# Normalised activations at 64, 192, 192 and 448 bytes from the weights' place, in place of 320

## The chip, the core and the metric

One core of a Trainium2 chip runs the whole program. The time is the device time of one execution in microseconds: 793.31 us for the kernel before, the median of 3 runs (793.28 to 793.38). All times below come from these runs or from one profiled execution of the same kernel.

## The reference

Input: 256 tokens of width 1024, float32, with 16 meta tokens put in front for the first mixer. Two blocks follow each other.

```python
# first block: h has 16 + 256 rows
a = rmsnorm(h, norm1); proj = a @ w_in           # pool, forgetting and stick-breaking attention
h = h + concat(y_pool, y_fox, y_sb) @ w_out
a = rmsnorm(h, norm2)                            # norm 0 below
h = h + (silu(a @ w_gate) * (a @ w_up)) @ w_down # first FFN, width 2816
h = rmsnorm(h, final_norm)
# second block
h = swiglu(rmsnorm(x, ffn1_pre), w_ffn1_in, w_ffn1_out)   # second FFN, norm 1
x = x + 0.5 * rmsnorm(h, ffn1_post)
h = mixer(rmsnorm(x, mix_pre), w_mix_in, ...)             # convolution and mLSTM, norm 2
x = x + rmsnorm(h, mix_post)
h = swiglu(rmsnorm(x, ffn2_pre), w_ffn2_in, w_ffn2_out)   # third FFN, norm 3
x = x + 0.5 * rmsnorm(h, ffn2_post)
```

## The kernel before

**Numbers in two parts.** Every large product is taken in a reduced float32 format (F32R) from a high and a low part. ScalarE rounds the landed weights `raw` into `whi` (L695), VectorE takes `wlo = raw - whi` (L1023). The activations have `xn_hi` and `xn_lo` in the same way. A product is then three: whi with hi, whi with lo, wlo with hi.

**The weight stream.** All large weights come as 129 units of 128 x 2048 values (1 MB), one after another into three slots (`raw`, `whi`, `wlo`, each three tiles of 8192 bytes per partition). SyncE issues the loads. An FFN has 11 groups of 256 hidden features with a gate, an up and a down unit each. The groups 2 to 10 run in a loop on every engine.

**The matmuls of a group.** Gate unit: 16 products of whi with 512 moving columns (hi and lo parts of 256 tokens side by side, `hi_products`), then 16 of wlo with 256 columns of hi (`lo_products`). Up unit: first its 16 wlo products, then its 16 whi products. So in order of time there are 16 of 512 columns, 32 of 256, 16 of 512. Down unit (`rows_tile`): 24 products of 512 columns, in which the hidden activations `hhi` and `hlo` are the stationary operand and the weights move. Each matmul has its own load of the stationary operand, which the profile shows as PEld. All of them are issued from the helper `mm`, L1478.

**The mixer.** 12 units. Ten are column products (`columns_tile`): for each k tile whi with hi, whi with lo, wlo with hi, 256 columns each. Two units, of kind v, have the activations as stationary operand and the weights moving (`tokens_tile`). Short work of the mLSTM heads stands between units. At the head of each FFN and of the mixer a first unit (`first_paired_unit`, `first_columns_unit`) runs all hi products and then all lo products as the activations arrive.

**Where the activations stand.** `xa` is one tile, 8 x 544 values per partition. In the first stage (projections, `w_in`) it is used as it is: k tile `kt` at 544 x 4 x kt = 2176 kt bytes, hi part first, lo part 1088 bytes on. For the three FFNs and the mixer the same memory is seen as 8 k tiles of 2 x 256 values, 2048 bytes apart, that start a given number of values into `xa`. `XN_AT` holds that number for norm 0 to 3, and L424 cuts the views from it:

```python
for at, far in XN_AT:
    line = xa_line[:, at:at + KT * 2 * SEQ if far == SEQ else at + 2 * far]
    if far == SEQ:
        xn.append(line.rearrange("p (k h c) -> p k h c", k=KT, h=2))
```

The tiles between `whi` and `xa` are whole multiples of 512 bytes, so `whi`, `wlo` and the start of `xa` have one address modulo 512. A stationary block of a column product begins at a multiple of 512 bytes in its slot. With 80 values, an activation block begins 320 bytes on from it, modulo 512, for every k tile. `ya`, `hhi` and `hlo` begin at 0 on the same scale.

Of the kernel before, what the change touches and what calls it, by code (L numbers as in the profile page):

```python
# [41 lines left out]
SEQ = 256  # L42
# [3 lines left out]
GROUPS = FF // 256  # L46
UNIT = 2048
SLOTS = 3
XN_AT = ((80, SEQ),) * 4
XN_HI = (0, 0, 0, 0)  # L50
EPS = 1e-6
NEG = -1e30
# [218 lines left out]
def build_blocks(nc, x_in, meta_in, wstream, ident_in, vecs_in, small_in, const_in, rows_in, out):  # L271
    with ExitStack() as ctx:  # L272
# [150 lines left out]
        xn = []  # L423
        for at, far in XN_AT:  # L424
            line = xa_line[:, at:at + KT * 2 * SEQ if far == SEQ else at + 2 * far]
# [1600 lines left out]
```

## Time and profile before

| | |
|---|---|
| median of 3 runs | 793.31 us |
| the profiled execution | 793.85 us, of which the span from first to last instruction 792.0 |
| TensorE busy | 781.6 us, 99% of the span |
| weight loads (PEld) busy | 687.9 us, 87% |
| VectorE, ScalarE busy | 533.2 us (67%), 429.3 us (54%) |
| granted TensorE clock | 1.000 of full |
| DMA | 141.16 MB, mean 178 GB/s |
| longest group | whi with xa, 1744 matmuls, 377.4 us busy |

In the stages: first stage to 120 us, first FFN loop some 148.6 to 304, second 331 to 486, mixer 504 to 600, third FFN loop 627 to 782. TensorE's rows give the start of an instruction and its length. The length includes the way through the array, so consecutive matmuls overlap in the view. The pace is the distance from one start to the next. A row with x16 holds 16 consecutive matmuls of one form, from the start of the first to the end of the last.

### The profile page before, as it was taken

Reading aid. Unit: us, or ns where it says so; the run is one execution under the profiler, and the core shown is the slowest. Engines: PE = TensorE matmul, PEld = TensorE weight load, DVE = VectorE, ACT = ScalarE, POOL = GpSimd, SP = SyncE. Lnnn points to the kernel's source line nnn. Section 1 sums busy time; section 2 is a strip of 40 time slices with the busy share of each in tenths; the row PEclk is TensorE's granted clock in tenths of the full one; section 3 lists DMA queues with packets and bytes.
Section 4 is the critical chain, followed back from the end, with each engine's and each line's share of the span. In section 5 each row is a group of like instructions: output and inputs, shape, how many; then the busy total and the mean of one; then the engine's idle time right before and its main releaser. Section 6 shows DMA issues by size and latency. Waiting matters only on the chain.

```text
span 792.0 us, 12209 instructions
## 1 busy us (share of the span) xinstructions
PE 781.6 (99%) x4710; PEld 687.9 (87%) x4710; DVE 533.2 (67%) x628; ACT 429.3 (54%) x565; POOL 28.3 (4%) x35
## 2 busy tenths in 40 slices
PE   9999999999999999999999999999999999999997
PEld 8989988888888888888888887999988888888885
DVE  7866657766666667866666566766977766666665
ACT  6556657544544448744544447565557654454444
POOL 0000000000000000000000000002520000000000
PEclk9999999999999999999999999999999999999999
DMA  9633433645555553665545554452444664555521
GB/s 335 235 110 112 143 115 128 245 166 205 191 183 209 175 196 110 238 224 199 198 176 209 183 188 159 142 204 108 161 165 162 221 223 166 205 192 183 208 106 54
DMA packets 20797, 141.16 MB, mean 178 GB/s; under 512 B 2448, under 2 KB 2704, under 8 KB 4384
## 3 DMA queue, kind: packets, MB, share of 16 engines
q1 hardware_dynamic: 20192, 138.65, 48.8%
q0 software_dynamic: 576, 2.10, 0.8%
q8 instruction: 21, 0.34, 0.2%
q14 instruction: 8, 0.07, 0.0%
HBM read 139.69 MB, written 1.05 MB: 178 GB/s over the span
## 4 chain that ended last, share of the span: by engine, by line
PE 94%; ACT 2%; DVE 2%; issue 1%; DMA 1%; SPq 0%; DVEq 0%; ACTq 0%
PE ps L1478 93%; ACT whi L695 1%; PE ps L1484 1%; DMA raw<-wstream 1%; DVE x L1227 0%; ACT squared L710 0%; DVE xa L1034 0%; PE ps L1707 0%; DVE wlo L1023 0%; PE ps L1677 0%; PE ps L1926 0%; DVE xg L1222 0%; DVEq L272 0%; ACT L928 0%; PE ps L1709 0%
## 5 line engine op out<-in xcount | busy, mean ns | idle before, releaser
L1478 PE MATMUL ps<-xa,whi 128*128 128x512 f32 (+2 forms) x1744 | 377.4, 347 | 0.0
L1023 DVE TENSOR_TENSOR wlo<-raw,whi 128x2048 fp32r<-128x2048 f32 x128 | 293.6, 2295 | 82.2 <-ACT whi L695 82.2
L1478 PEld LDWEIGHTS ps<-xa,whi 128*128 128x128 f32 x1744 | 299.6, 188 | 41.4 <-issue 2.1
L695 ACT ACTIVATE whi<-raw 128x2048 fp32r<-128x2048 f32 x128 | 244.2, 1909 | 6.9 <-PE ps L1478 6.8
L1478 PE MATMUL ps<-xa,wlo 128*128 128x256 f32 (+1 forms) x1376 | 219.8, 278 | 0.0
L1478 PEld LDWEIGHTS ps<-xa,wlo 128*128 128x128 f32 x1376 | 187.9, 188 | 2.8
L1478 PE MATMUL ps<-wlo,hhi 128*128 128x512 f32 x240 | 93.5, 390 | 0.0
L1478 PE MATMUL ps<-whi,hlo 128*128 128x512 f32 x240 | 93.5, 390 | 0.0
L1478 PE MATMUL ps<-whi,hhi 128*128 128x512 f32 x240 | 93.5, 390 | 0.0
L889 ACT ACTIVATE hhi<-arena 128x512 fp32r<-128x512 f32 x30 | 19.0, 633 | 88.4 <-PE ps L1478 81.9
L875 ACT ACTIVATE arena<-ps 128x512 f32<-128x512 f32 x33 | 19.7, 597 | 85.5 <-PE ps L1478 85.4
L883 ACT ACTIVATE arena<-ps 128x512 f32<-128x512 f32 x33 | 19.7, 597 | 71.4 <-PE ps L1478 71.4
L1478 PE MATMUL ps<-whi,ya 128*128 128x512 f32 x176 | 56.5, 395 | 0.0
L1478 PEld LDWEIGHTS ps<-whi,hhi 128*128 128x128 f32 x240 | 45.1, 188 | 9.6
L1478 PEld LDWEIGHTS ps<-wlo,hhi 128*128 128x128 f32 x240 | 45.1, 188 | 9.5
L1478 PEld LDWEIGHTS ps<-whi,hlo 128*128 128x128 f32 x240 | 45.1, 188 | 9.5
L1269 DVE TENSOR_TENSOR arena<-ps,arena 128x512 f32<-128x512 f32 x33 | 22.8, 691 | 39.6 <-ACT arena L875 39.6
L1278 DVE TENSOR_TENSOR arena<-ps,arena 128x512 f32<-128x512 f32 x33 | 22.8, 691 | 36.6 <-ACT arena L883 36.6
L1290 DVE TENSOR_TENSOR hlo<-arena,hhi 128x512 fp32r<-128x512 f32 x30 | 20.8, 692 | 37.8 <-ACT hhi L889 37.7
L1478 PEld LDWEIGHTS ps<-whi,ya 128*128 128x128 f32 x176 | 33.1, 188 | 6.8
L1478 PE MATMUL ps<-wlo,ya 128*128 128x512 f32 x88 | 34.5, 393 | 0.0
L1478 PE MATMUL ps<-arena 64*128 64x144 f32 (+11 forms) x190 | 24.3, 340 | 1.8 <-DVE arena L1067 1.3
(221 smaller groups left out, 531.6 us busy)
## 6 DMA issues: line engine op xcount, KB each, us to landing
raw<-wstream SPq DMA_DIRECT2D x128, 1024.0 KB, 4.8
gain_row<-rows_in POOLq DMA_DIRECT2D x4, 512.0 KB, 3.9
x<-x_in SPq DMA_DIRECT2D x2, 512.0 KB, 4.0
raw<-wstream SPq DMA_DIRECT2D x2, 512.0 KB, 5.8
out<-x SPq DMA_DIRECT2D x4, 256.0 KB, 2.1
xg<-const_in SPq DMA_DIRECT2D x1, 912.0 KB, 11.8
small<-small_in SPq DMA_DIRECT2D x1, 152.0 KB, 6.1
arena<-meta_in SPq DMA_DIRECT2D x1, 64.0 KB, 4.5
```

Of the source, the lines that this page charges most:

```text
L695: nc.scalar.activation(whi[slot][:], raw[slot][:], ACT.Copy).then_inc(hi_ready, 1)
L875: nc.scalar.activation(silu, products(4)[1], ACT.Copy).then_inc(gate_lo_out, 1)
L883: nc.scalar.activation(up_sum, products(6)[1], ACT.Copy).then_inc(up_lo_out, 1)
L889: nc.scalar.activation(ya[:, 0:2, 0:SEQ] if last else hhi[:], hact, ACT.Copy).then_inc(hhi_done, 1)
L1023: nc.vector.tensor_tensor(wlo[slot][:], raw[slot][:], whi[slot][:].bitcast(F32), ALU.subtract).then_inc(lo_ready, 1)
L1269: nc.vector.tensor_tensor(silu, products(4)[0], silu, ALU.add).then_inc(gate_out, 1)
L1278: nc.vector.tensor_tensor(up_sum, products(6)[0], up_sum, ALU.add).then_inc(up_out, 1)
L1290: nc.vector.tensor_tensor(lo, hact, hi.bitcast(F32), ALU.subtract).then_inc(hlo_done, 1)
L1478: return nc.tensor.matmul(o, lhsT, rhs, start=start, stop=stop, skip_group_check=True)
L1484: ins = nc.tensor.transpose(turn_place(k, kt)[:, tt * P:(tt + 1) * P], x[:, tt, kt * P:(kt + 1) * P], ident[:])
```

## The change

`XN_AT` gets other numbers. Norm 0 (first FFN) begins 16 values = 64 bytes into `xa`, norm 1 (second FFN) 48 values = 192 bytes, norm 2 (mixer) 192 bytes, norm 3 (third FFN) 112 values = 448 bytes, in place of 320 bytes for all four. The widest view still ends inside the tile (112 + 4096 of 4352 values). The order of instructions on every engine is the same in both kernels; only addresses of reads and writes in `xa` differ.

```diff
-XN_AT = ((80, SEQ),) * 4
+XN_AT = ((16, SEQ), (48, SEQ), (48, SEQ), (112, SEQ))
 XN_HI = (0, 0, 0, 0)
```

## Rows read from the trace of the kernel before

**Rows 1.** The page: busy time, share and instructions; granted clock; chain by engine.
```profile
PE 781.6 (99%) x4710; PEld 687.9 (87%) x4710; DVE 533.2 (67%) x628; ACT 429.3 (54%) x565; POOL 28.3 (4%) x35
...
PEclk9999999999999999999999999999999999999999
...
PE 94%; ACT 2%; DVE 2%; issue 1%; DMA 1%; SPq 0%; DVEq 0%; ACTq 0%
```

**Rows 2.** Window 331 to 486 us, FFN two's loop: busy us by engine, then clock.
```profile
331.00:486.00 155.00, 155.00 (x825) 133.17 (x825) 99.82 (x80) 76.19 (x70) 0.00 (x0) 1.00 0.55 196
```

**Rows 3.** TensorE in order of time (start us, length us), FFN two, group 2.
```profile
338.14 3.84 PE L1478 MATMUL ps<-xa,whi 128*128 128x512 f32 x16
341.82 3.79 PE L1478 MATMUL ps<-xa,wlo 128*128 128x256 f32 x32
345.44 3.82 PE L1478 MATMUL ps<-xa,whi 128*128 128x512 f32 x16
349.10 0.39 PE L1478 MATMUL ps<-whi,hhi 128*128 128x512 f32 x1
...
351.16 0.39 PE L1478 MATMUL ps<-whi,hhi 128*128 128x512 f32 x1
...
354.33 0.39 PE L1478 MATMUL ps<-whi,hlo 128*128 128x512 f32 x1
```

**Rows 4.** The same view, mixer, a unit of column products.
```profile
524.80 0.28 PE L1478 MATMUL ps<-xa,wlo 128*128 128x256 f32 x1
...
526.92 0.28 PE L1478 MATMUL ps<-xa,wlo 128*128 128x256 f32 x1
```

**Rows 5.** The same view, the mixer's two v units.
```profile
511.07 0.28 PE L1478 MATMUL ps<-wlo,xa 128*128 128x256 f32 x1
...
511.78 0.28 PE L1478 MATMUL ps<-wlo,xa 128*128 128x256 f32 x1
...
518.06 0.28 PE L1478 MATMUL ps<-wlo,xa 128*128 128x256 f32 x1
...
518.74 0.28 PE L1478 MATMUL ps<-wlo,xa 128*128 128x256 f32 x1
```

**Rows 6.** The same view, mixer's first unit, then the third FFN's first units.
```profile
499.06 1.98 PE L1478 MATMUL ps<-xa,whi 128*128 128x256 f32 x16
...
608.65 2.05 PE L1478 MATMUL ps<-xa,whi 128*128 128x256 f32 x16
...
612.52 5.66 PE L1478 MATMUL ps<-xa,whi 128*128 128x512 f32 x24
...
620.31 3.93 PE L1478 MATMUL ps<-xa,wlo 128*128 128x256 f32 x32
```

**Rows 7.** TensorE's busy us and instructions (x) in 4 us windows, mixer.
```profile
517.50:521.50 4.00, 4.00 (x38) 1.00 0.12 16
...
552.00:556.00 4.00, 4.00 (x36) 1.00 0.33 117
```

**Rows 8.** TensorE in order of time, first stage, four k tiles' whi pairs.
```profile
32.40 0.41 PE L1478 MATMUL ps<-xa,whi 128*128 128x272 f32 x2
...
32.77 0.42 PE L1478 MATMUL ps<-xa,whi 128*128 128x272 f32 x2
...
33.16 0.41 PE L1478 MATMUL ps<-xa,whi 128*128 128x272 f32 x2
...
33.53 0.42 PE L1478 MATMUL ps<-xa,whi 128*128 128x272 f32 x2
```

**Rows 9.** Groups by form, TensorE: loops of FFN two, three, then mixer.
```profile
L1478 PE MATMUL ps<-xa,whi 128*128 128x512 f32 x296 | 71.0, 392 | 0.0
...
L1478 PE MATMUL ps<-xa,whi 128*128 128x512 f32 x292 | 70.1, 392 | 0.0
...
L1478 PE MATMUL ps<-xa,whi 128*128 128x256 f32 x288 | 52.2, 283 | 0.0
L1478 PE MATMUL ps<-xa,wlo 128*128 128x256 f32 x144 | 40.2, 279 | 0.0
```

## The prediction

> **What bounds the kernel now.** I read the busy times and the clock first, then the chain of waits, then TensorE's instructions in order of time. TensorE is busy 99% of the span at the full granted clock, 2.4 GHz by the row's nines, and the chain lies 94% on it [rows 1]. Inside the loop of the second FFN it never pauses, 155.0 us busy of 155.0 [rows 2], and the other two loops read the same. So neither transfers nor the other engines set the end there. What a matmul costs beside the next one does, and that is the only thing an address can change.
>
> I take that cost from start to start, since the duration shown holds the drain as well. Group 2 of the second FFN [rows 3]: the 16 gate products with whi start at 338.14 and the next kind at 341.82, 3.68/16 = 230 ns each; the 16 up products take 349.10 - 345.44 = 3.66, 228.8 each; mean 229.4 for 512 columns. The 32 products with wlo take 3.62/32 = 113.1 ns for 256 columns. The 14 down products from 351.16 to 354.33 take 226.4 each. By columns, 113.3 and 226.7 look like one floor, and the whi products stand 2.7 ns above it. The third FFN shows the same lengths.
>
> The mixer is different. From 524.80 to 526.92 there are 18 products of 256 columns, 2.12/18 = 117.8 ns each, 4.5 above the floor [rows 4]. The v units show both: 511.07 to 511.78 is 118 each, 518.06 to 518.74 is 113 each, the same instructions and shapes, in two slots whose places differ by whole multiples of 512 bytes [rows 5]. So one pair of addresses has two paces, and what went before decides. The same is seen ahead of the FFNs: 16 whi products take 1.98 us in one place and 2.05 in another, (1.98 - 0.28)/15 = 113.3 and (2.05 - 0.28)/15 = 118.0 [rows 6]. The slow pace is inherited: group 1 of the third FFN has its 32 wlo products in 3.93 us, (3.93 - 0.28)/31 = 117.7, although 32 products of 512 columns stand just ahead; in group 2, behind the first down products, they take 3.79 [rows 3, 6]. In the mixer most stretches are slow: a window of 4 us holds 36 products (four windows, 36 or 37 each), and 38 in the fast v unit and in the first unit [rows 7], the two or so under way at the edge counted.
>
> **Does the address matter, and by what period?** While matmuls stream, the loads of the next weights are under way, 87% of the span [rows 1]: two reads of SBUF side by side. In the first stage each k tile stands 2176 bytes behind the last, so the moving operand's place changes by 128 bytes modulo 256 and also modulo 512. Its pairs of whi products read 0.41, 0.42, 0.41, 0.42 us and so on, alternately over the eight tiles, of which four stand in the rows, and a tile of three products takes 0.37 or 0.39 us in turn [rows 8]. Place therefore matters, with a period of two tiles: 256 bytes, not 512. Then 320 and 64 are one place, and 192 and 448 are one place. This step is read from hundredths of a microsecond, so I hold it at four in five.
>
> **The change part by part.** No instruction, wait or DMA is added, removed or moved. ScalarE and VectorE write the normalised activations to other columns of the same tile, in pieces of the same shape.
> (a) First FFN, 320 to 64: one place by the period. 0.
> (b) Second and third FFN, 320 to 192 modulo 256. Their loops hold 296 + 292 = 588 whi products of 512 columns [rows 9]. No row has such a product at 192. Bounds: the down products' floor, 588 x 2.7 = 1.6 us gained; on the other side, the 16 gate products behind a down unit take 19 ns more than the 16 up products (16 x 1.2), which four openers at some 234 ns would make (an estimate: 229.4 + 19/4); if that pace held throughout, 588 x 4.6 = 2.7 us lost. I take most of the gain, 1.2, because the nearest steady rows at 512 columns are the down products.
> (c) Their 576 wlo products (18 groups of 32 as in rows 3) already run at the floor and cannot gain. If the new place made them inherit the slow pace they would lose 576 x 4.5 = 2.6 us. I take 0, since a down unit at distance 0 still stands ahead of each gate unit, and behind it the products were fast.
> (d) Mixer: 432 of the column products (288 + 144) [rows 9] at 4.5 ns above the floor are 1.9 us. The only rows with operands 192 apart are the v units, which have activations as weights and weights as the moving operand, 64 the other way round: one unit fast, one slow [rows 5]. Half, 0.95. Bounds: all of it gained; or the fast v unit turned slow (48 x 4.5 = 0.2) and each column product as slow as the worse tiles of the first stage, where three products of 272 columns take 0.39 us [rows 8], 130 each against a floor of 120.4, 9.6 above it and 5.1 worse than now: 0.2 + 2.2 = 2.4 lost.
> (e) The openings of the second and third FFN hold some 96 slow products each, 96 x 4.5 = 0.4 us each ([rows 6] show the third's). I leave them, and keep 0.8 for the range.
> Sum: 1.2 + 0.95 = 2.15 us gained. The profiled execution took 793.85 (span 792.0 and 1.85 around it), 0.54 above the median of the runs, 793.31. With the change 791.7 on its own scale, 791.2 on the median's. All bounds of gain together are 1.6 + 1.9 + 0.8 = 4.3, to 789.0.
>
> The Trainium skill speaks against all of this. Its page "TensorE: Matmul & The Clock Gate", section "Step-by-step: what each phase is for", says that TensorE has two independent read ports to SBUF and that loading the next weights takes nothing from the running matmul; "SBUF — State Buffer", section "SBUF: two separate sides", adds that TensorE never waits on anyone there. By that rule the sum would be 0 and the time 793.3. Rows 5 and 8 disagree in part: something in the pair of reads changes a matmul by 4 to 5 ns. They do not show that 192 is better than 64.
>
> **The rivals.**
> A, no effect: only the distance's being an odd multiple of 64 counts, 64 and 192 are mirror images and the two paces go on as they fall. For it: the period of 256, and the v units, which at the mirrored distance have just the two paces that the column products have at 64. Against it: whi products at 64 have a pace of their own (229.4) between the others, which need not be symmetric. Time 793.3, within 0.5 of it. This is also the case that the change does not do what it says, certain for the first FFN if the period holds.
> B, slower: at 192 the wlo products of the second and third FFN lock into the slow pace, as group 1 of the third FFN does today. Place: behind the gate's 16 whi products in each of the 18 loop groups. Price: 2.6 us for (c), with (b) and (d) unchanged: 795.9. It decides from the point where a row of 32 wlo products reads 3.93 instead of 3.79. Against it: the rows in between are wiped clean by each down unit today.
> C, the period is 512 after all, and the first FFN changes too: its loop holds the same 0.8 us above the floor, so with the forecast's gains 790.4.
>
> **How the numbers follow.** A measurement of this kernel tells about 0.2%, 1.6 us, from no change. Forecast case (part of (b) and (d) gained, 789.0 to 792.6): 0.44, of which 0.06 falls short of 1.6 us. C 0.08, faster. A 0.28. B 0.20, of which 0.02 is within 1.6 us. So faster 0.38 + 0.08 = 0.46, same 0.06 + 0.28 + 0.02 = 0.36, slower 0.18. The likeliest time is 791.2. The range is 789.0, all gains, to 796.0, B's price; the forecast case alone is 789.0 to 792.6. Beyond 796.0 lie B together with the losses of (b) and (d).
>
> **What the profile after would show.** The first FFN's rows unchanged: 3.84, 3.79, 3.82 us for 16, 32 and 16 products, or C is right. In the second and third FFN the whi rows at 3.79 to 3.80 in place of 3.84 and 3.82 for (b); the wlo row stays 3.79 or goes to 3.93 (B). In the mixer 38 products in 4 us where 36 or 37 stood for (d). I am wrong in kind if any engine but TensorE shows a changed wait, or if whi products get slower than 229.4 ns.

## The result and the profile after

The changed kernel takes 795.86 us (median of 6 runs, 795.65 to 796.39), the kernel before in the same comparison 793.60 (6 runs, 793.28 to 794.24). The ratio is 1.0029, with a 95% interval of 1.0018 to 1.0039. It is slower by some 2.3 us, where 2.15 us faster was forecast. The profiled execution took 796.36 us with a span of 794.6, which is 2.6 more than the 792.0 of before.

The page of the changed kernel, against [rows 1]: busy times and shares, granted clock, and the chain by engine.

```profile
PE 783.2 (99%) x4710; PEld 686.1 (86%) x4710; DVE 533.3 (67%) x628; ACT 429.4 (54%) x565; POOL 28.3 (4%) x35
...
PEclk9999999999999999999999999999999999999999
...
PE 89%; DVE 6%; ACT 2%; issue 1%; DMA 1%; SPq 0%; POOL 0%; DVEq 0%; ACTq 0%
```

The clock is the same. The chain has moved: PE has 89% of it and DVE 6%, where it was 94% and 2%. TensorE is busy 1.6 us more.

Where the time went is read from four starts of the same matmuls. TensorE in order of time, the kernel before (start us, length us, then the instruction): first product of the second FFN, of the mixer, of the third FFN, and the last product with wlo.

```profile
310.74 0.36 PE L1478 MATMUL ps<-xa,whi 128*128 128x256 f32 x1
...
495.36 0.35 PE L1478 MATMUL ps<-xa,whi 128*128 128x256 f32 x1
...
604.80 0.36 PE L1478 MATMUL ps<-xa,whi 128*128 128x256 f32 x1
...
785.77 0.39 PE L1478 MATMUL ps<-wlo,ya 128*128 128x512 f32 x1
```

The same four in the changed kernel.

```profile
310.99 0.37 PE L1478 MATMUL ps<-xa,whi 128*128 128x256 f32 x1
...
497.01 0.36 PE L1478 MATMUL ps<-xa,whi 128*128 128x256 f32 x1
...
606.16 0.36 PE L1478 MATMUL ps<-xa,whi 128*128 128x256 f32 x1
...
788.36 0.39 PE L1478 MATMUL ps<-wlo,ya 128*128 128x512 f32 x1
```

The differences are 0.25, 1.65, 1.36 and 2.59 us. The first 0.25 is there before any activation of the change is read: the stages up to the first FFN differ by it, and the whole first FFN adds 0.00. The second FFN adds 1.40, the mixer gives back 0.29, the third FFN adds 1.23.

TensorE in order of time in the changed kernel, a group in the loop of the first FFN and group 2 of the second, with the first down product behind each, to be read against [rows 3].

```profile
155.02 3.84 PE L1478 MATMUL ps<-xa,whi 128*128 128x512 f32 x16
158.70 3.79 PE L1478 MATMUL ps<-xa,wlo 128*128 128x256 f32 x32
162.33 3.82 PE L1478 MATMUL ps<-xa,whi 128*128 128x512 f32 x16
165.99 0.39 PE L1478 MATMUL ps<-whi,hhi 128*128 128x512 f32 x1
...
338.54 3.89 PE L1478 MATMUL ps<-xa,whi 128*128 128x512 f32 x16
342.27 3.80 PE L1478 MATMUL ps<-xa,wlo 128*128 128x256 f32 x32
345.91 3.89 PE L1478 MATMUL ps<-xa,whi 128*128 128x512 f32 x16
349.64 0.40 PE L1478 MATMUL ps<-whi,hhi 128*128 128x512 f32 x1
```

First FFN, 64 bytes: 3.84, 3.79, 3.82 as before, and 10.97 us from the first product to the down unit. Second FFN, 192 bytes: 3.89, 3.80, 3.89 and 11.10 us. The 16 whi products take (342.27 - 338.54)/16 = 233.1 ns, and (349.64 - 345.91)/16 = 233.1 ns, where they took 230.0 and 228.8. The row of the 32 wlo products is 0.01 us longer. The third FFN, at 448 bytes, has the same 11.10 us.

The mixer in the changed kernel, same view: the last 16 products of its first unit (whi with the lo part), two places in each v unit, and two 1.70 us apart in a unit of column products.

```profile
500.86 2.05 PE L1478 MATMUL ps<-xa,whi 128*128 128x256 f32 x16
...
512.54 0.28 PE L1478 MATMUL ps<-wlo,xa 128*128 128x256 f32 x1
...
513.25 0.28 PE L1478 MATMUL ps<-wlo,xa 128*128 128x256 f32 x1
...
519.66 0.28 PE L1478 MATMUL ps<-wlo,xa 128*128 128x256 f32 x1
...
520.36 0.28 PE L1478 MATMUL ps<-wlo,xa 128*128 128x256 f32 x1
...
526.21 0.28 PE L1478 MATMUL ps<-xa,wlo 128*128 128x256 f32 x1
...
527.91 0.28 PE L1478 MATMUL ps<-xa,wlo 128*128 128x256 f32 x1
```

It is close to the mirror of [rows 4 to 6]: the column products are fast, the first unit and the second v unit slow; the first v unit was slow before as well. The column products run at (527.91 - 526.21)/15 = 113.3 ns. Both v units run at 118 ns, (513.25 - 512.54)/6 and (520.36 - 519.66)/6, and so does the first unit, 2.05 us for 16. TensorE's waits from 560 to 580 us show where the gain went (engine and line, what it waited for, us in total, times, longest).

```profile
PE ps L1478 <- DVE arena L1389: 0.5, 1, 0.5
PE ps L1478 <- DVE arena L1395: 0.2, 1, 0.2
```

The kernel before has no such wait in that stretch. The longer of the two, TensorE in order of time, first the kernel before, then the changed one:

```profile
577.25 0.60 PE L1926 MATMUL ps<-ident,arena 128*128 128x128 f32 x4
577.61 0.48 PE L1478 MATMUL ps<-whi,ya 128*128 128x512 f32 x1
```

```profile
577.83 0.60 PE L1926 MATMUL ps<-ident,arena 128*128 128x128 f32 x4
578.97 0.50 PE L1478 MATMUL ps<-whi,ya 128*128 128x512 f32 x1 [0.54 <-DVE arena L1389]
```

From start to start it is 0.36 us before and 1.14 after, 0.78 more; the place of the other wait costs 0.31 more. Added up in this way over the whole mixer, the column products take 1.7 us less, the v units 0.3 more and the work between the units 1.1 more. That leaves the 0.29 us.

### The profile page after: what moved, and what is told of

Its sections match the earlier page's. It is cut to its first block, busy times and chain, and to the rows that moved or that the text cites. A ratio compares the mean times of both kernels' runs of the same rounds, so it can differ in the third digit from the quotient of the medians.

```text
span 794.6 us, 12209 instructions
## 1 busy us (share of the span) xinstructions
PE 783.2 (99%) x4710; PEld 686.1 (86%) x4710; DVE 533.3 (67%) x628; ACT 429.4 (54%) x565; POOL 28.3 (4%) x35
## 4 chain that ended last, share of the span: by engine, by line
PE 89%; DVE 6%; ACT 2%; issue 1%; DMA 1%; SPq 0%; POOL 0%; DVEq 0%; ACTq 0%
PE ps L1478 87%; DVE wlo L1023 2%; ACT whi L695 1%; DMA raw<-wstream 1%; PE ps L1484 1%; DVE arena L1444 0%; DVE arena L1455 0%; DVE x L1227 0%; ACT squared L710 0%; DVE xa L1034 0%; PE ps L1707 0%; PE ps L1677 0%; POOL arena L671 0%; DVE ya L1043 0%; DVE arena L1383 0%
```

## Experiments

The distance below is that of the activations from the weights' place, modulo 256 unless it is said otherwise. The loop group is the 64 products of a gate and an up unit, from the first start to the start of the down unit: 10.97 us at 320, 11.10 at 192.

**The mixer alone at 192.**

```diff
-XN_AT = ((80, SEQ),) * 4
+XN_AT = ((80, SEQ), (80, SEQ), (48, SEQ), (80, SEQ))
```

> The three FFNs stay at 320 bytes, the mixer alone goes to 192. Theory 1 (the whi products of 512 columns in the second and third FFN carry the whole loss, and the mixer's gain is given back at waits on VectorE): the mixer's column products run at 113.3 ns, its v units at 118, TensorE waits 0.3 and 0.8 us more on VectorE's L1395 and L1389, and the time is 0 to 0.5 us under the kernel before. Rival (the mixer itself is slower for its waits): 0.5 to 1.5 us over it. Rival (the gain of 1.9 us shows in full once the FFNs are left alone): 1.5 us or more under it.

Measured 793.64 us against 793.69, ratio 0.9998 (0.9989 to 1.0007). TensorE in order of time, second FFN:

```profile
338.26 3.84 PE L1478 MATMUL ps<-xa,whi 128*128 128x512 f32 x16
...
349.23 0.39 PE L1478 MATMUL ps<-whi,hhi 128*128 128x512 f32 x1
```

A wait of TensorE from 494 to 604 us in the same run, beside 2.0 us on `x` that the kernel before has too:

```profile
PE ps L1478 <- DVE arena L1389: 0.5, 1, 0.5
```

The FFN is back at 10.97 us. The mixer has its fast column products (113.3 ns), slow v units (118) and the wait on L1389. So the mixer's part of the change is worth nothing that can be measured, as theory 1 said, and the gain in pace does not become time.

The same run shows something about the two paces. Up to the mixer its instructions and addresses are those of the kernel before. The last 16 products of the first unit of the first FFN, first in the kernel before, then in this run:

```profile
130.19 1.98 PE L1478 MATMUL ps<-xa,whi 128*128 128x256 f32 x16
```

```profile
130.44 2.05 PE L1478 MATMUL ps<-xa,whi 128*128 128x256 f32 x16
```

That is (1.98 - 0.28)/15 = 113.3 ns in one execution and (2.05 - 0.28)/15 = 118.0 in the other. So not even the order of the work together with the addresses fixes which of the two paces is taken in an opening. In the loops all nine groups of an FFN agree within 0.01 us in every run.

**The second and third FFN alone at 192.**

```diff
-XN_AT = ((80, SEQ),) * 4
+XN_AT = ((80, SEQ), (48, SEQ), (80, SEQ), (48, SEQ))
```

> Second and third FFN at 192 bytes, first FFN and mixer at 320 as before. Theory (whi products of 512 columns at 192 carry the whole loss): 11.10 us per group of 64 products in both FFNs, in all 2.4 to 2.9 us over the kernel before, ratio 1.003; the mixer's rows as before. Rival (part of the loss comes from the mixer's new state or from the openings): under 1.5 us over.

Measured 796.91 us against 793.75, ratio 1.0036 (1.0023 to 1.0050). Both FFNs are at 11.10 us per group (second FFN, same view):

```profile
338.10 3.89 PE L1478 MATMUL ps<-xa,whi 128*128 128x512 f32 x16
...
349.20 0.40 PE L1478 MATMUL ps<-whi,hhi 128*128 128x512 f32 x1
```

The two FFNs carry the whole loss; the mixer, from its first product to the third FFN's, takes 109.5 us against 109.4 in the kernel before. The medians differ by 3.2 us, a little over the 2.4 to 2.9 expected; the interval, 1.8 to 4.0 us, holds those. The profiled spans differ by the same 2.6 us as the full change.

**Distance or absolute place.**

```diff
-XN_AT = ((80, SEQ),) * 4
+XN_AT = ((48, SEQ), (48, SEQ), (48, SEQ), (48, SEQ))
+        pad = sb("pad", [P, 32])          # 128 bytes, ahead of whi
         whi = [sb(f"whi{s}", [P, UNIT], F32R) for s in range(SLOTS)]
```

> All four norms at 192 bytes, and an unused tile of 128 bytes ahead of whi, so that weights and activations all stand 128 bytes further on: the activations are at the absolute address modulo 512 that they have at 320 in the kernel before, while the distance is 192. Theory 1 (distance): all three FFN loops at 11.10 us per group of 64 products, whi products at 233.3 ns, time 796.5 to 797. Rival (the absolute place of the moving operand): 10.97 us and 229 ns as in the kernel before, time 793.5.

One run, 797.36 us. A loop group of the first FFN:

```profile
154.69 3.89 PE L1479 MATMUL ps<-xa,whi 128*128 128x512 f32 x16
158.43 3.80 PE L1479 MATMUL ps<-xa,wlo 128*128 128x256 f32 x32
...
165.79 0.40 PE L1479 MATMUL ps<-whi,hhi 128*128 128x512 f32 x1
```

165.79 - 154.69 = 11.10 us, and the whi products take (158.43 - 154.69)/16 = 233.8 ns (233.3 over the nine groups). The other two loops read the same. The activations stood at the address modulo 512 of the kernel before, the weights 128 bytes further on. What counts is the distance, not the place of the activations. 192 and 448 give the same paces, as 320 and 64 do: the period of 256 holds.

**Other distances.** Three runs change `XN_AT` alone: (0, 32, 0, 8) values, (24, 40, 32, 56) and (12, 20, 52, 18).

> First FFN at 0 bytes, second at 128, mixer at 0, third at 32. A loop group's 64 products take 10.97 us at 64 and 11.10 at 192. Theory 1 (the distance of moving from stationary place, modulo 256, sets the pace, with the down products at 0 as the floor): 226.7 ns per product of 512 columns and 10.89 us per group in the first FFN; 128 is open, 10.9 to 11.3; 32, half a step from 0, between the first FFN's value and 10.97. Rival (whi products with hi and lo parts side by side are slower for a reason of their own, and only that differs from the down products): 229 ns in the first FFN as well, 10.97 us. Mixer: theory 1 says 113.3 ns where the pace is not inherited slow.

> First FFN at 96 bytes, second at 160, mixer at 128, third at 224. If the pace rises smoothly with the distance from 64 (229.0 ns) to 192 (233.3), 96 and 160 lie between them, 10.97 to 11.10 us per group of 64 products, and 224 lies over or under 192 as the curve goes back to 0. If only the whole 64-byte block counts, 96 reads as 64 (10.97), 160 as 128 and 224 as 192 (11.10).

> First FFN at 48 bytes, second at 80, mixer at 208, third at 72 from both weights' places. 64 has 10.97 us per group of 64 products, 32 and 96 had 11.24 and 11.32. If 64 is the bottom of a smooth curve, 48, 72 and 80 lie between, 10.97 to 11.3. If only places at a whole 64 bytes are good, all three are at 11.2 to 11.3 us at once. A value under 10.97 would give a better kernel.

| distance, bytes | run | loop group, us |
|---|---|---|
| 0 | first FFN of the first | 11.11 |
| 32 | third FFN of the first | 11.24 |
| 48 | first FFN of the third | 11.26 |
| 64 | kernel before | 10.97 |
| 72 | third FFN of the third | 11.25 |
| 80 | second FFN of the third | 11.24 |
| 96 | first FFN of the second | 11.32 |
| 128 | second FFN of the first | 11.26 |
| 160 | second FFN of the second | 11.24 |
| 192 | changed kernel | 11.10 |
| 224 | third FFN of the second | 11.24 |

They took 801.87, 803.97 and 802.69 us, one run each. There is no curve between 64 and 192, and no neighbour of 64 is good: 48 and 72 are already at the level of 128. The smooth curve of the expectations is out, and so is the reading that every whole 64 bytes is good, since 128 is not. So 64 was the best place of the eleven, and the change had only one way to go in the FFNs. The mixer at distance 0 missed too: its column products take 120.0 ns, where theory 1 had 113.3. The first FFN at distance 0:

```profile
154.86 3.79 PE L1478 MATMUL ps<-xa,whi 128*128 128x512 f32 x16
158.48 4.00 PE L1478 MATMUL ps<-xa,wlo 128*128 128x256 f32 x32
162.31 3.82 PE L1478 MATMUL ps<-xa,whi 128*128 128x512 f32 x16
165.97 0.39 PE L1478 MATMUL ps<-whi,hhi 128*128 128x512 f32 x1
```

The first 16 whi products take (158.48 - 154.86)/16 = 226.3 ns, the floor, as theory 1 said. The other 16, behind the wlo products, take (165.97 - 162.31)/16 = 228.8, as at 64: their first five take 229 to 235 ns, the rest 226 to 227. The 32 wlo products take (162.31 - 158.48)/32 = 119.7 ns, over 6 more than at 64, which I had not foreseen: the group is 0.14 us slower, not 0.08 faster. So the two kinds of product do not have the same best place.

**whi at 0 and wlo at 64.** The last finding suggests a layout with both at their best.

```diff
-XN_AT = ((80, SEQ),) * 4
+XN_AT = ((0, SEQ), (0, SEQ), (80, SEQ), (0, SEQ))
+        pad_lo = sb("pad_lo", [P, 48])    # 192 bytes
         wlo = [sb(f"wlo{s}", [P, UNIT], F32R) for s in range(SLOTS)]
+        pad_xa = sb("pad_xa", [P, 16])    # 64 bytes
```

> wlo is moved by a 192-byte pad ahead of it, and a 64-byte pad behind it puts xa back on whi's place. The three FFNs' activations stand at 0 from whi and at 64 from wlo; the mixer's at 64 from whi and 128 from wlo. Theory (what counts is the distance, modulo 256, of the moving operand from the stationary operand that is being loaded for the next matmul, pair by pair): the whi products of 512 columns run at 226.7 ns as at 0, the wlo products of 256 at 113.3 as at 64 where they do not inherit the slow pace; the down products, whose moving weights alternate between distance 0 (whi) and 192 (wlo), rise from 226.7 to 228 to 229 ns. A group's 64 products take 10.88 us (10.97 before), the 24 down products 5.45 to 5.50; the mixer's columns are slow, 118 to 120 ns. Time 790.5 to 793.5. Rival (the pace is a property of the activations' place against whi alone): wlo products at 119.8 as at 0, 11.11 us per group, time 798 or more.

Measured 799.39 us, ratio 1.0064 (1.0046 to 1.0083). A loop group of the first FFN:

```profile
155.05 3.83 PE L1480 MATMUL ps<-xa,whi 128*128 128x512 f32 x16
158.72 3.93 PE L1480 MATMUL ps<-xa,wlo 128*128 128x256 f32 x32
162.49 3.84 PE L1480 MATMUL ps<-xa,whi 128*128 128x512 f32 x16
166.16 0.39 PE L1480 MATMUL ps<-whi,hhi 128*128 128x512 f32 x1
```

The wlo products take (162.49 - 158.72)/32 = 117.8 ns. That is neither the 113.3 of the theory nor the rival's 119.7. It equals the slow pace that products at 64 also have, in [rows 4 and 6]; that it is the same state is not shown. The whi products do reach 226 to 227 ns, but only after some ten matmuls at 224 to 236. The down products, whose moving weights are no longer all at distance 0, are not the cause of that: the second 16 whi products open in the same way behind wlo products. The expected 790.5 to 793.5 us was missed by 6. A table of places, pair by pair, does not predict a sequence.

**The second half of the moving operand.**

```diff
-XN_AT = ((80, SEQ),) * 4
+XN_AT = ((80, 2048 + 48), (80, 2048), (80, SEQ), (80, 2048 + 32))
```

> The hi parts of all norms stay at distance 64. The lo parts, the second 256 of the 512 moving columns, stand in a line of their own: in the first FFN at distance 0, in the second at distance 64 (a control for the other layout, k tiles 1024 bytes apart), in the third at 192. If the meeting of the two reads falls in the first half of a moving operand (the weight load is 128 columns long and begins with the matmul), the lo part's place changes nothing: 229 ns and 10.97 us per group in all three. If it reaches into the second half, the first FFN gets nearer to 226.7 ns (10.89 us) and the third nearer to 233 (11.10).

One run, 798.40 us. TensorE in order of time, the first FFN (lo part at 0), then the second (lo part at 64, the control):

```profile
154.80 3.90 PE L1478 MATMUL ps<-xa,whi 128*128 128x512 f32 x16
158.53 3.93 PE L1478 MATMUL ps<-xa,wlo 128*128 128x256 f32 x32
162.30 3.89 PE L1478 MATMUL ps<-xa,whi 128*128 128x512 f32 x16
166.03 0.39 PE L1478 MATMUL ps<-whi,hhi 128*128 128x512 f32 x1
...
340.74 3.84 PE L1478 MATMUL ps<-xa,whi 128*128 128x512 f32 x16
...
351.71 0.39 PE L1478 MATMUL ps<-whi,hhi 128*128 128x512 f32 x1
```

The control is equal to the kernel before, 351.71 - 340.74 = 10.97 us, so the layout itself is free. With the lo part at 0 the whi products take (158.53 - 154.80)/16 = 233.1 ns, and the wlo products, whose own operands and places are untouched, (162.30 - 158.53)/32 = 117.8. The third FFN, with the lo part at 192, is at 11.19 us. The first reading, that only the first half meets the load, falls. The second had the effect but not its direction: 0 made it worse. And a change in the whi products alone moved the wlo products from the fast pace to the slow one. The step between the two halves of a moving operand changed together with the lo part's place, and this run does not tell the two apart.

**What takes the mixer's gain back.** In both runs the scaling of the mLSTM weights `pw` by VectorE is left out. These are 8 operations (L1455) of 0.35 to 0.83 us, 4.2 us in all, and not the 6 us of the expectations; VectorE's busy time falls by 2.5 us, from 533.2 to 530.7, as other operations take longer. The mixer stands at 320 in the first and at 192 in the second.

```diff
-                    for tt in range(TT):
-                        link(nc.vector.tensor_scalar(pw[:, tt, :], pw[:, tt, :], ...))
```

> All norms at 320 bytes as before. Left out: VectorE's scaling of the mLSTM weights pw in the mixer (L1455, two operations of 0.8 us for each of four heads), so that VectorE's chain is some 6 us shorter there. Theory (in the mixer with activations at 64 TensorE's own pace sets the time): no change of more than 0.3 us from the kernel before, since TensorE waited for VectorE nowhere between 504 and 600 us. Rival (VectorE sets the mixer's time already): 1 us or more faster.

> Mixer at 192 bytes, FFNs at 320, and the same operations of VectorE left out as in the run with the mixer at 64. Theory (at 192 the column products gain 1.6 us and the v units lose 0.2, and VectorE takes the rest back): without its load TensorE does not wait on L1389 and L1395, and the time is 1.0 to 1.5 us under the run with the mixer at 64. Rival (the waits come from something else, a transfer or ScalarE): the waits of 0.5 and 0.2 us stay and the two light runs agree within 0.4 us.

Measured 793.93 us (ratio to the kernel before 0.9996, 0.9986 to 1.0005) and 792.61 (0.9983, 0.9974 to 0.9993). The spans of the two (us from first to last instruction, granted clock), first at 320, then at 192:

```profile
core 0: 791.5 us, clock 0.999
```

```profile
core 0: 790.1 us, clock 0.999
```

The only wait of TensorE from 494 to 604 us in the second:

```profile
PE ps L1481 <- DVE x L1227: 2.0, 3, 0.9
```

At 320 the lighter VectorE changes nothing. At 192 the waits on L1389 and L1395 are gone and the time is 1.3 to 1.4 us under that at 320. In the real kernel VectorE is therefore the next bound of the mixer, some 0.3 us behind TensorE.

## Why the prediction was wrong

(a) Right. The first FFN adds 0.00 us, its rows are those of [rows 3], and C is out.

(b) This step failed. The text read: "No row has such a product at 192", and then took 1.2 us of gain "because the nearest steady rows at 512 columns are the down products". Measured, the whi products at 192 take 233.1 ns, 3.7 over the 229.4 at 64. 588 of them make 2.2 us lost, inside the bound of 2.7 that the step had named for the other side. The down products were near only in their columns. Their distance is 0, and 0 and 192 are different places: a gate unit's whi products at 0 do run at 226.3. For the sum this step alone is an error of 3.4 us of the 4.4 between forecast and result. The runs on the FFNs alone and on the mixer alone confirm that it decides. Why 192 is slower than 64 stays open.

(c) Right to 0.2 us. The wlo rows went from 3.79 to 3.80 us in each of the 18 groups, and did not take the slow pace.

(d) Right in sign and kind of effect for the pace, wrong for the time. The column products gained 1.7 of the 1.9 us, so that half of it was too little, and the v units lost 0.3. But only 0.29 us left the mixer, where 0.95 was in the sum. This step failed as well: it took a gain in TensorE's pace for a gain in time and put nothing for the waits on VectorE, which cost 1.1 us. VectorE becomes the bound there after some 0.3 us, and the two light runs show it.

(e) As left: the wlo unit of the third FFN's opening became fast, that of the second's stayed slow, the mixer's first unit became slow, and nothing over 0.2 us came of any of them.

Rival A is out: 64 and 192 are not mirror images for products of 512 columns. Rival B had the right time, 795.9, by luck. The loss sits in the loops of the second and third FFN, as it said, but in the whi products, and its price was for another thing. Its sign, 3.93 in place of 3.79 for the wlo row, did not appear. The sign that I had given for being wrong in kind, whi products over 229.4 ns, did.

The Trainium skill, "TensorE: Matmul & The Clock Gate", section "Step-by-step: what each phase is for", says that TensorE reads SBUF through two independent ports, so that loading the next weights takes no bandwidth from the running matmul. The rule that followed from it, no effect of the place, does not hold here: the same 64 products take 10.97 to 11.32 us with nothing changed but the distance between the two operands. Whether that arises at the ports no run shows.

## What to carry to other kernels

A term that the trace does not show at the new setting must not be filled in from a row that shares the shape and differs in the very thing that is changed. Take it as open on both sides, and let the rival on the other side weigh as much. Where a stream of F32R matmuls is back to back and fully busy, the distance modulo 256 bytes of moving from stationary operand is worth a sweep in steps of 64 bytes, measured in place, because a pace found for one sequence did not carry over to another here. And a gain in TensorE's pace needs the next engine's slack in that stage first.

## What the runs showed of the hardware

- The pace of back-to-back F32R matmuls at the full clock depends on the distance modulo 256 bytes between the moving operand and the stationary ones: 226.3 to 234 ns for 512 columns, 113.3 to 120 for 256. Moving both by 128 bytes, at the distance 192, changes nothing.
- The best place is not the same for two shapes: at 0 the 512-column products are fastest (226.3 ns behind down products, 228.8 behind wlo products) and the 256-column ones slow (119.7); at 64 they are at 229.4 and 113.3.
- 256-column products at one distance have two paces, 113.3 and 118 ns, and hold one of them over units of 48 matmuls and more. In the last layout run a change of the products ahead switched it. In the first unit of the first FFN two executions whose instructions and addresses are the same up to there took different ones (1.98 and 2.05 us for 16).
- Why the distance counts with this period, and what decides which pace is taken, stays open. No run changed the stationary load itself.
- No layout of those tried beats the kernel before. The nearest is the mixer alone at 192, ratio 0.9998.
